# Stores of sums issued by ScalarE's queue instead of GpSimd's, in a two-block transformer kernel on one Trainium2 core

## The chip, the core and the metric

The kernel runs on one core of one Trainium2 chip. The core has five engines that run their own instruction streams and meet at semaphores: TensorE (PE: matmuls and transposes), VectorE (DVE), ScalarE (ACT), GpSimd (POOL) and SyncE (SP). SP, ACT and POOL can each issue DMA transfers, which then run beside the engines. The metric is the time of one execution on the device in microseconds (us), as the median of several runs; lower is better.

## What is computed

Two transformer blocks follow one another on one sequence of 256 tokens with 2048 features, in float32. The first has three mixers side by side (sparse, windowed and block attention), each with its own output matrix and gate, and an MLP; the second has two layers of two mixers each (differential and banded attention, then grouped and latent attention) with 256 more context tokens. What matters here is the shape of the large products:

```
h = rms_norm(x, norm_mix[layer])
... = jnp.split(h @ w_in[layer], SPLIT_POINTS, axis=-1)
y = jnp.einsum('bsmc,mcd->bsmd', branches, w_branch[layer])
x = x + jnp.sum(gate * y, axis=2) @ w_out[layer]
x = x + jnp.square(jax.nn.relu(h @ w_mlp_in[layer])) @ w_mlp_out[layer]
...
u = h @ e_w_in[i]          # second block, layer 0
u = h @ o_w_in[i]          # second block, layer 1
x = x + gate * (y @ w_o[l])
```

## The kernel before

**Steps and chunks.** All large products are `Step`s: 512 (or 472, 320) columns of a weight matrix, in chunks of two rows of 128 (`wcols`), against two or four tiles of 128 tokens. A step with two tiles uses two of the PSUM banks 0 to 3, one with four all of them. Float32 accuracy comes from three matmuls of split operands (lines 525, 529, 530): for each chunk SP loads `raw` (line 416, eight buffers), ScalarE copies it rounded to `w_hi` (`split_hi`, line 428, four buffers), VectorE subtracts to get `w_lo` (`split_lo`, line 434), and TensorE multiplies. ScalarE may write a `w_hi` buffer once TensorE has used the chunk four earlier, so both splitters can be up to three chunks ahead. A chunk is 12 matmuls with two tiles and 24 with four.

**Where the sums go.** Most projections (qkv, gates, in2, in3, and the small products QB and KVB) are steps of kind "store": ScalarE copies each tile's bank from PSUM to one of four buffers in SBUF (`act_evac`, line 577), and GpSimd stores the buffer to DRAM (`pool_store`, line 674), to U1, U2 or U3 (all read as U in the profile), GT, QB, KVB or MODP. Before the copy ScalarE waits for `acc_done` or `w_used` (TensorE has filled the bank) and for `stored` (the buffer's last store has landed); the copy's end raises `acc_free`, for which both GpSimd's store and TensorE's next use of the bank wait.

```
nc.scalar.activation(stage_bufs[bank][0:r, 0:s.width], acc[0:r, bank, 0:s.width],
                     e["func"], scale=e["scale"](tt) if callable(e["scale"]) else e["scale"])\
  .then_inc(acc_free[bank], 1)
```

**The order of the work.** Each engine's order is written out. `stream` (line 637) sets ScalarE's and VectorE's in a stage: the copies of the last step come behind the split of the third chunk of the next step in the stages named in `LATE`, and otherwise, and at each end of a stage, between the splits of the first and the second chunk of what follows. In the attention regions (`Region`, line 988) the products of a stage fill the gaps of small work units: TensorE makes scores, VectorE the maximum, ScalarE the exponential (`pb`, line 1242) and, two units later, a copy of the transposed result (`pt`, line 1251); `Region.act` puts the copies of a finished step ahead of a unit's exponential, and `Region.pool` GpSimd's stores at the same unit. The Silu of the later gates needs another table in ScalarE than the exponential, so there a table load stands on either side of the copies. Between in3 and what follows, the feed `p8q` (line 779, `a_hi`) comes right behind the copies. GpSimd has other work in the same queue: loads of gates and attention results for the next stage, reciprocal roots, and the saves of attention results.

Of the kernel before, what the change touches and what calls it, by code (L numbers as in the profile page):

```python
# [124 lines left out]
def two_blocks(nc, A, C, out):  # L125
    ctx = ExitStack()
    with ctx:
# [127 lines left out]
        stages = {}  # L255
# [9 lines left out]
        gates = [group(win, QKV1 + j * G, alternate(j == 0), x256, store(to(GT, j * G), ACT.Tanh, rms(2))) for j in range(12)]  # L265
# [299 lines left out]
        def act_evac(act, s):  # L565
            e = s.evac
            for bank, tt in s.tiles:
                if e["kind"] == "store":
                    wait_done(act, s, bank)
                    if s.put[bank]:  # L570
                        act.wait_ge(stored[bank], 16 * s.put[bank])
                    r = e["rows"]
                    if e.get("gates"):
                        c0 = e["gates"]
                        nc.scalar.activation(nsa_g[:, tt, :], acc[:, bank, c0:c0 + 24], ACT.Tanh, scale=rms(2)(tt))\
                          .then_inc(nsa_ready, 1)
# [3 lines that stand above are left out]
                elif e["kind"] == "relu2":  # L580
                    wait_done(act, s, bank)
                    if tt == 0:
                        act.wait_ge(ht_done, s.nth)
                    nc.scalar.activation(relu_t[:, tt, :], acc[:, bank, :], ACT.Relu, scale=rms(4)(tt))\  # L584
                      .then_inc(acc_free[bank], 1)

        def act_hidden(act, s):
            act.wait_ge(ht_done, s.nth + 1)
# [78 lines left out]
        def dve_stream(dve, st):  # L667
            stream(dve, st, split_lo, dve_evac, dve_hidden, "dve")

        def pool_store(pool, s):  # L670
            e = s.evac
            for bank, tt in s.tiles:
                pool.wait_ge(acc_free[bank], s.fill[bank] + 1)
                pool.dma_start(e["dst"](tt, s.width), stage_bufs[bank][0:e["rows"], 0:s.width])\  # L674
                    .then_inc(stored[bank], 16)
            if e.get("gates"):
                pool.wait_ge(nsa_ready, 2)
                pool.dma_start(AG.rearrange("(t p) n -> p t n", p=P), nsa_g[:, :, :]).then_inc(nsa_out, 16)

# [5 lines left out]
        def pool_stream(pool, st):  # L685
            if st.name == "branch":
                for s in st.steps:
                    q, n, m = s.nth, s.evac["n"], s.evac["m"]
                    if q >= 2:
                        pool.wait_ge(branch_tmp, 2 * (q - 1))  # L690
                    for tt in range(2):
                        pool.dma_start(gate_t[:, q % 2, tt, :], GT[tt * P:(tt + 1) * P, m * DM + n * G:m * DM + (n + 1) * G])\
                            .then_inc(gate_in[q % 2], 16)
                    if q == 3:
                        f2.turned(pool, f2.n - 1)
                        vec_bias(pool, 2)
                    vec_mods(pool, s)
                return
            for i, s in enumerate(st.steps):
                vec_mods(pool, s)  # L700
                if s.evac["kind"] == "relu2":
                    for bank, tt in s.tiles:
                        pool.wait_ge(acc_free[bank], s.fill[bank] + 1)
                        last = nc.gpsimd.tensor_tensor(relu_t[:, tt, :], relu_t[:, tt, :], relu_t[:, tt, :], ALU.mult)  # L704
                    last.then_inc(sq_done, 1)
                elif s.evac["kind"] == "store":
                    pool_store(pool, s)
                st.run_hooks("pool", i, 0, pool)

        def wait_stored(eng, upto):  # L710
# [277 lines left out]
        class Region:  # L988
# [100 lines left out]
            def pool(self, pool):  # L1089
                stored_here = []  # L1090
                for p in self.passes:
                    waiting = p.gate
                    for x in p.row_places + ["units"] + list(range(p.U + 3)):
                        for f in p.pool_parts.get(x, ()):
                            f(pool)
                        for s_ in self.finished(p, x):
                            pool_store(pool, s_)
                            stored_here.append(s_)
                        if waiting and (waiting[0] not in self.stage.steps or waiting[0] in stored_here):
                            for bank, _ in waiting[0].tiles:  # L1100
                                pool.wait_ge(stored[bank], 16 * (waiting[0].put[bank] + 1))
                            pool.dma_start(waiting[1], waiting[2]).then_inc(gate_there, 16)
                            waiting = None
# [1361 lines left out]
        def _(pool):  # L2465
# [28 lines left out]
            out2_roots(pool, 1, 0)  # L2494
            pool_stream(pool, stages["in3_low"])
            p8_pool(pool)
            pool_store(pool, stages["in3"].steps[0])
            p8_pool_norm(pool)
            for s_ in stages["in3"].steps[1:]:
                pool_store(pool, s_)  # L2500
            pool_stream(pool, stages["in3_g0"])
            C0.roots(pool)
            at3.pool(pool)
# [146 lines left out]
```

## Time and profile before

| | before |
|---|---|
| median of 3 runs | 3244.88 us (3236.37 to 3247.44) |
| the profiled execution | 3239.18 us, span 3237.4 us |
| granted clock of TensorE, mean | 0.984 |
| TensorE busy | 3137.8 us, 97% |
| VectorE busy | 1949.3 us, 60% |
| ScalarE busy | 1323.3 us, 41% |
| GpSimd busy | 234.1 us, 7% |
| stores issued on line 674, by destination | U 98, GT 24, KVB 16, QB 6, MODP 4: 148 |
| DMA moved | 620.53 MB, 192 GB/s in the mean |

The engines overlap, so the shares don't add up. A matmul's records overlap too, so that "97% busy" says that TensorE nearly always had a matmul under way and not that the array was at its peak. In the rows, L434 is line 434 of the kernel; `w_lo<-raw,w_hi` are the tensors written and read; ACTq and SPq are the queues in which these engines issue DMAs; "[0.26 <-DVE w_lo L434]" says that the engine was idle for 0.26 us before, until VectorE's line 434 released it. A granted clock of 1.00 is 2.4 GHz.

### The profile page before, as it was taken

What the parts mean: (1) busy time and instruction counts of PE and PEld (TensorE: products, weight loads), DVE (VectorE), ACT (ScalarE), POOL (GpSimd) and SP (SyncE); (2) the same over time, 40 slices, a digit from 0 to 9 for tenths busy, and PEclk for the clock granted to TensorE, in tenths of its full rate; (3) what the DMA queues carried; (4) which work ended last, traced back from release to release, by engine and by line L of the source; (5) the groups of instructions that cost most, each with busy time, mean ns of one, the idle gap of its engine ahead of it and who ended that gap; (6) DMA issues with size and microseconds to landing.
All of it is one profiled execution on the core that took longest, in us unless ns stands there. A gap on an engine that the chain in (4) does not pass through costs nothing.

```text
span 3237.4 us, 38936 instructions
## 1 busy us (share of the span) xinstructions
PE 3137.8 (97%) x14876; PEld 2553.0 (79%) x14876; DVE 1949.3 (60%) x2669; ACT 1323.3 (41%) x2084; POOL 234.1 (7%) x323
## 2 busy tenths in 40 slices
PE   8999999999999999999989999999999999999988
PEld 7887888888888888888878877777778878777666
DVE  5767555568769888887657433444445436355555
ACT  4443444443344343434543233333343324244553
POOL 1000000000001010100100000000001000020000
PEclk9999999999999999999999999999999999999999
DMA  8977855457768877897745522422435424464663
GB/s 243 346 255 258 269 177 168 143 181 270 258 206 271 270 254 261 267 257 254 235 145 176 163 80 94 142 65 101 129 103 198 133 83 134 162 215 128 211 231 133
DMA packets 319717, 620.53 MB, mean 192 GB/s; under 512 B 29515, under 2 KB 96456, under 8 KB 318636
## 3 DMA queue, kind: packets, MB, share of 16 engines
q1 hardware_dynamic: 296684, 544.74, 52.3%
q0 software_dynamic: 19600, 66.89, 6.0%
q10 hardware_dynamic: 3248, 6.42, 0.5%
q8 instruction: 119, 1.95, 0.3%
q14 instruction: 66, 0.54, 0.1%
HBM read 575.16 MB, written 49.08 MB: 193 GB/s over the span
## 4 chain that ended last, share of the span: by engine, by line
PE 87%; DVE 4%; DMA 4%; ACT 2%; issue 2%; POOL 1%; SPq 0%; ACTq 0%; POOLq 0%; DVEq 0%
PE acc L525 25%; PE acc L530 24%; PE acc L529 24%; PE acc L1180 4%; PE acc L1207 3%; PE acc L1195 2%; DVE w_lo L434 2%; DMA raw<-in_w_in 1%; PE acc L818 1%; PE acc L496 1%; PE acc L1184 1%; ACT w_hi L428 1%; PE acc L1164 1%; DMA QB<-stage 0%; PE acc L557 0%
## 5 line engine op out<-in xcount | busy, mean ns | idle before, releaser
L525 PE MATMUL acc<-w_hi,a_hi 128*128 128x512 f32 (+4 forms) x3800 | 1514.1, 398 | 22.8 <-DVE w_lo L434 13.7
L530 PE MATMUL acc<-w_hi,a_lo 128*128 128x512 f32 (+4 forms) x3800 | 1478.0, 389 | 0.0
L529 PE MATMUL acc<-w_lo,a_hi 128*128 128x512 f32 (+4 forms) x3800 | 1476.8, 389 | 0.0
L434 DVE TENSOR_TENSOR w_lo<-raw,w_hi 128x1024 fp32r<-128x1024 f32 (+3 forms) x826 | 984.5, 1208 | 439.2 <-ACT w_hi L428 427.5
L428 ACT ACTIVATE w_hi<-raw 128x1024 fp32r<-128x1024 f32 (+3 forms) x826 | 855.6, 1046 | 808.9 <-PE acc L530 757.4
L525 PEld LDWEIGHTS acc<-w_hi,a_hi 128*128 128x128 f32 x3800 | 723.7, 190 | 173.6 <-DVE w_lo L434 24.1
L530 PEld LDWEIGHTS acc<-w_hi,a_lo 128*128 128x128 f32 x3800 | 722.5, 190 | 146.2
L529 PEld LDWEIGHTS acc<-w_lo,a_hi 128*128 128x128 f32 x3800 | 723.9, 191 | 131.6 <-issue 1.0
L1321 DVE TENSOR_REDUCE at_st<-acc 128x1 f32<-128x256 f32 (+3 forms) x208 | 101.2, 487 | 423.0 <-PE acc L1180 282.2
L1242 ACT ACTIVATE pb<-acc,at_st 128x256 f32<-128x256 f32 (+3 forms) x208 | 108.3, 521 | 374.9 <-DVE at_st L1321 351.4
L469 DVE SCALAR_TENSOR_TENSOR lanes_b<-raw,ct,lanes_b 128x1024 f32<-128x1024 f32 x150 | 190.3, 1310 | 0.3 <-DMA raw<-in_w_mod 0.3
L469 DVE SCALAR_TENSOR_TENSOR lanes_c<-raw,ct,lanes_c 128x1024 f32<-128x1024 f32 x120 | 159.2, 1370 | 0.0
L674 POOL DMA_DIRECT2D U<-stage x98 | 53.3, 546 | 990.4 <-ACT stage L577 862.4
L1195 PEld LDWEIGHTS acc<-ident,pb 128*128 128x128 f32 (+1 forms) x528 | 63.4, 142 | 66.8 <-issue 58.9
L1251 ACT ACTIVATE pt<-acc 128x256 f32<-128x256 f32 (+3 forms) x208 | 89.5, 430 | 60.5 <-PE acc L1195 60.5
L1195 PE MATMUL acc<-ident,pb 128*128 128x128 f32 (+1 forms) x528 | 96.2, 281 | 10.7 <-ACT pt L1251 10.5
L577 ACT ACTIVATE stage<-acc 128x512 f32<-128x512 f32 (+2 forms) x100 | 55.1, 593 | 99.8 <-PE acc L530 86.4
L704 POOL TENSOR_TENSOR relu_t<-relu_t 128x512 f32<-128x512 f32 x32 | 56.4, 1772 | 495.5 <-ACT relu_t L584 495.5
L1298 DVE RECIPROCAL at_st<-at_st 128x1 f32<-128x1 f32 x208 | 33.9, 163 | 83.4 <-PE acc L1207 78.2
L859 DVE TENSOR_TENSOR a_lo<-acc,a_hi 128x512 fp32r<-128x512 f32 x76 | 51.9, 690 | 38.3 <-ACT a_hi L841 36.5
L1180 PE MATMUL acc<-kAT,qAT 64*128 64x512 f32 (+1 forms) x128 | 58.2, 534 | 0.0
L841 ACT ACTIVATE a_hi<-acc 128x512 fp32r<-128x512 f32 x44 | 25.6, 597 | 78.8 <-PE acc L818 78.8
(392 smaller groups left out, 1833.7 us busy)
## 6 DMA issues: line engine op xcount, KB each, us to landing
raw<-in_w_mod SPq DMA_DIRECT2D x192, 512.0 KB, 4.9
raw<-in_w_mlp_in SPq DMA_DIRECT2D x128, 512.0 KB, 4.1
raw<-in_w_mlp_out SPq DMA_DIRECT2D x128, 512.0 KB, 5.5
raw<-in_e_w_in SPq DMA_DIRECT2D x104, 512.0 KB, 5.1
raw<-in_w_in SPq DMA_DIRECT2D x96, 512.0 KB, 5.0
raw<-in_w_in SPq DMA_DIRECT2D x88, 472.0 KB, 5.7
raw<-in_w_o SPq DMA_DIRECT2D x64, 512.0 KB, 4.9
raw<-in_o_w_in SPq DMA_DIRECT2D x64, 512.0 KB, 4.3
```

The costliest lines, as they stand in the source:

```text
L428: nc.scalar.activation(w_hi[:, n % SPLITS, 0:size], raw[:, r % RAWS, 0:size], ACT.Copy)\
L434: nc.vector.tensor_tensor(w_lo[:, n % SPLITS, 0:size], raw[:, r % RAWS, 0:size], w_hi[:, n % SPLITS, 0:size].bitcast(F32), ALU.subtract)\
L469: nc.vector.scalar_tensor_tensor(out=t, in0=raw[:, vecs.raw[q] % RAWS, :], scalar=ct[:, k, v:v + 1], in1=bias_of(j)[:, :] if k == 0 else t ...
L525: nc.tensor.matmul(o, s.lhs(0, kt, tt), wh, start=kt == 0, stop=False)
L529: nc.tensor.matmul(o, s.lhs(0, kt, tt), wl, start=False, stop=False)
L530: last = nc.tensor.matmul(o, s.lhs(1, kt, tt), wh, start=False, stop=end)
L1180: last = nc.tensor.matmul(acc[:, bank, 0:w.keys], w.q[x], w.k[x], start=x == 0, stop=x == n - 1 and w.bias is None)
L1195: last = nc.tensor.transpose(acc[0:kk, bank, x * P:(x + 1) * P], self.pb[:, v % self.npb, x * P:x * P + kk], ident[:, :])
L1207: last = nc.tensor.matmul(acc[:, self.obanks[v % len(self.obanks)], 0:P], self.pt[0:kk, v % 2, x, :], vt, start=x == 0, stop=x == len(w.v) ...
L1242: nc.scalar.activation(self.pb[:, v % self.npb, 0:w.keys], acc[:, 4 + v % 2, 0:w.keys], ACT.Exp, bias=st[:, 0:1], accum_out=st[:, 1:2]).th ...
L1251: nc.scalar.activation(self.pt[0:kk, v % 2, 0:n, :], acc[0:kk, self.tbanks[v % len(self.tbanks)], 0:n * P].rearrange("p (n t) -> p n t", n ...
L1321: ins = nc.vector.tensor_reduce(m, acc[:, 4 + v % 2, 0:w.keys], AX.X, ALU.max, negate=True)
```

## The change

The stores of a step are issued by ScalarE, behind all the copies of that step, and no longer by GpSimd. The waits, the transfers and the buffers are the same. GpSimd keeps the one extra store of a step with `gates`. The new function stands ahead of the lines of before, so that line n of `Region` and of all below is n + 4 afterwards; the new store is line 593.

```diff
                     nc.scalar.activation(relu_t[:, tt, :], acc[:, bank, :], ACT.Relu, scale=rms(4)(tt))\
                       .then_inc(acc_free[bank], 1)
+            if e["kind"] == "store":
+                act_store(act, s)
+
+        def act_store(act, s):
+            e = s.evac
+            for bank, tt in s.tiles:
+                act.wait_ge(acc_free[bank], s.fill[bank] + 1)
+                act.dma_start(e["dst"](tt, s.width), stage_bufs[bank][0:e["rows"], 0:s.width])\
+                    .then_inc(stored[bank], 16)
...
-        def pool_store(pool, s):
-            e = s.evac
-            for bank, tt in s.tiles:
-                pool.wait_ge(acc_free[bank], s.fill[bank] + 1)
-                pool.dma_start(e["dst"](tt, s.width), stage_bufs[bank][0:e["rows"], 0:s.width])\
-                    .then_inc(stored[bank], 16)
-            if e.get("gates"):
+        def pool_gates(pool, s):
+            if s.evac.get("gates"):
                 pool.wait_ge(nsa_ready, 2)
                 pool.dma_start(AG.rearrange("(t p) n -> p t n", p=P), nsa_g[:, :, :]).then_inc(nsa_out, 16)
...
-                    pool_store(pool, s)
+                    pool_gates(pool, s)
...
-                            pool_store(pool, s_)
+                            pool_gates(pool, s_)
```

The two direct calls behind stage in3 on GpSimd are renamed in the same way.

ScalarE where stage qkv ends and qkv_end begins, before. `w_hi` of 128x928 belongs to qkv_end, whose first chunk is split ahead of the copies; in brackets are the semaphores that the row waits for.

```order
L428 ACTIVATE w_hi<-raw 128x928 [waits w_used,landed0]
L577 ACTIVATE stage<-acc,small 128x472 [waits stored2,acc_done2]
L577 ACTIVATE stage<-acc,small 128x472 [waits stored3,w_used]
L428 ACTIVATE w_hi<-raw 128x928 [waits w_used,landed2]
L428 ACTIVATE w_hi<-raw 128x928 [waits w_used,landed3]
```

The same place afterwards:

```order
L428 ACTIVATE w_hi<-raw 128x928 [waits w_used,landed0]
L577 ACTIVATE stage<-acc,small 128x472 [waits stored2,acc_done2]
L577 ACTIVATE stage<-acc,small 128x472 [waits stored3,w_used]
L593 DMA U<-stage 128x472 [waits acc_free2]
L593 DMA U<-stage 128x472 [waits acc_free3]
L428 ACTIVATE w_hi<-raw 128x928 [waits w_used,landed2]
L428 ACTIVATE w_hi<-raw 128x928 [waits w_used,landed3]
```

Two issues, each with a wait for ScalarE's own copy, now stand ahead of the split of the second chunk.

ScalarE in the second attention region, at a gate step with four tiles and Silu, before:

```order
L577 ACT_TABLE_LOAD [waits stored2]
L577 ACTIVATE stage<-acc 128x512 [waits acc_done2]
L577 ACTIVATE stage<-acc 128x512 [waits stored3,acc_done3]
L577 ACTIVATE stage<-acc 128x512 [waits stored0,acc_done0]
L577 ACTIVATE stage<-acc 128x512 [waits stored1,w_used]
L1241 ACT_TABLE_LOAD [waits at_t_done]
L1241 ACTIVATE at_st<-sinkB,at_st 128x1 [waits at_m_done]
```

And afterwards:

```order
L577 ACTIVATE stage<-acc 128x512 [waits stored1,w_used]
L593 DMA U<-stage 128x512 [waits acc_free2]
L593 DMA U<-stage 128x512 [waits acc_free3]
L593 DMA U<-stage 128x512 [waits acc_free0]
L593 DMA U<-stage 128x512 [waits acc_free1]
L1245 ACT_TABLE_LOAD [waits at_t_done]
L1245 ACTIVATE at_st<-sinkB,at_st 128x1 [waits at_m_done]
```

Four issues stand between the last copy and the table load for the exponential (line 1241 before, 1245 now).

ScalarE where the products QB end and KVB begin, before:

```order
L577 ACTIVATE stage<-acc 128x512 [waits stored0,acc_done0]
L577 ACTIVATE stage<-acc 128x512 [waits stored1,w_used]
L577 ACTIVATE stage<-acc 128x512 [waits stored2,acc_done2]
L577 ACTIVATE stage<-acc 128x512 [waits stored3,acc_done3]
L577 ACTIVATE stage<-acc 128x512 [waits stored0,acc_done0]
L577 ACTIVATE stage<-acc 128x512 [waits stored1,w_used]
L1242 ACT_TABLE_LOAD [waits at_t_done]
```

And afterwards:

```order
L593 DMA QB<-stage 128x512 [waits acc_free0]
L593 DMA QB<-stage 128x512 [waits acc_free1]
L577 ACTIVATE stage<-acc 128x512 [waits stored2,acc_done2]
L577 ACTIVATE stage<-acc 128x512 [waits stored3,acc_done3]
L577 ACTIVATE stage<-acc 128x512 [waits stored0,acc_done0]
L577 ACTIVATE stage<-acc 128x512 [waits stored1,w_used]
L593 DMA KVB<-stage 128x512 [waits acc_free2]
L593 DMA KVB<-stage 128x512 [waits acc_free3]
L593 DMA KVB<-stage 128x512 [waits acc_free0]
L593 DMA KVB<-stage 128x512 [waits acc_free1]
L1246 ACT_TABLE_LOAD [waits at_t_done]
```

The store of bank 2 now follows the copy of bank 1, which itself waits until the store of QB from bank 1 has landed.

## Rows read from the trace of the kernel before

**Rows 1.** The page, part 1: busy time and its share of the span.
```profile
PE 3137.8 (97%) x14876; PEld 2553.0 (79%) x14876; DVE 1949.3 (60%) x2669; ACT 1323.3 (41%) x2084; POOL 234.1 (7%) x323
```

**Rows 2.** Waits of TensorE: line, releaser, us in total, times, longest.
```profile
PE acc L525 <- DVE w_lo L434: 13.7, 18, 2.4
...
PE acc L525 <- ACT stage L577: 8.4, 8, 2.7
```

**Rows 3.** Line 674: duration min/median/max; its waiters; then DMA issues, KB, us to landing.
```profile
L674 POOL DMA_DIRECT2D U<-stage x98: 539/540/642, 40.3 to 3042.4; - x98
...
  ACT stage L577: 12.4, 7
...
out<-XR SPq DMA_DIRECT2D x4, 512.0 KB, 3.9
...
QB<-stage POOLq DMA_DIRECT2D x6, 256.0 KB, 6.2
```

**Rows 4.** Issues on the queues of ScalarE and SP; timeline of ScalarE, 79 to 82.
```profile
L1352 ACTq DMA_DIRECT2D onehot_t<-const_onehot x1: 467/467/467, 1.2 to 1.2; - x1
...
L1116 SPq DMA_DIRECT2D kA<-U x4: 501/1045/1685, 1835.3 to 2086.2; - x4
...
79.38 1.00 ACT L428 ACTIVATE w_hi<-raw 128x944 fp32r<-128x944 f32 x1 [1.58 <-PE acc L530]
79.40 0.86 ACTq L1444 DMA_DIRECT2D BROW<-BREV  x1
81.95 0.99 ACT L428 ACTIVATE w_hi<-raw 128x944 fp32r<-128x944 f32 x1 [1.58 <-PE acc L530]
```

**Rows 5.** Timelines around 264, then TensorE at 43 and 2861.
```profile
263.10 0.65 ACT L577 ACTIVATE stage<-acc,small 128x472 f32<-128x472 f32 x1 [0.63 <-PE acc L530]
263.66 3.57 ACT L428 ACTIVATE w_hi<-raw 128x928 fp32r<-128x928 f32 x4
...
264.05 0.54 POOL L674 DMA_DIRECT2D U<-stage  x1 [0.75 <-ACT stage L577]
...
265.84 0.48 PE L525 MATMUL acc<-w_hi,a_hi 128*128 128x464 f32 x1 [0.26 <-DVE w_lo L434]
...
43.35 0.48 PE L525 MATMUL acc<-w_hi,a_hi 128*128 128x472 f32 x1 [0.40 <-DVE w_lo L434]
...
2861.03 0.50 PE L525 MATMUL acc<-w_hi,a_hi 128*128 128x512 f32 x1 [0.18 <-DVE w_lo L434]
```

**Rows 6.** Timelines of ScalarE and TensorE, 2347 to 2353, a step with Silu.
```profile
2347.28 2.07 ACT L577 ACTIVATE stage<-acc 128x512 f32<-128x512 f32 x4
2349.37 1.28 ACT L1241 ACT_TABLE_LOAD   x1
...
2352.98 0.63 PE L1195 MATMUL acc<-ident,pb 128*128 128x128 f32 x4 [2.21 <-ACT pt L1251]
```

**Rows 7.** Timelines of ScalarE and TensorE, 2830 to 2833.
```profile
2830.40 1.08 ACT L779 ACTIVATE a_hi<-acc 128x512 fp32r<-128x512 f32 x2
...
2832.57 0.63 PE L770 MATMUL acc<-ident,lr 128*128 128x128 f32 x4 [2.01 <-DVE a_lo L787]
```

**Rows 8.** Timelines where QB and KVB are made, ScalarE, then TensorE.
```profile
2885.53 0.60 ACT L577 ACTIVATE stage<-acc 128x512 f32<-128x512 f32 x1 [0.82 <-PE acc L530]
...
2892.88 1.28 ACT L1242 ACT_TABLE_LOAD   x1
...
2872.89 0.47 PE L525 MATMUL acc<-w_hi,a_hi 128*128 128x512 f32 x1 [1.34 <-ACT stage L577]
...
2898.55 0.47 PE L525 MATMUL acc<-w_hi,a_hi 128*128 128x512 f32 x1 [0.44 <-ACT stage L577]
```

**Rows 9.** Stretches of 10 us (PEclk is the granted clock); TensorE at 2953.
```profile
2350.00:2360.00 10.00, 7.79 (x45) 6.19 (x44) 4.01 (x11) 5.23 (x14) 0.33 (x1) 1.00 0.22 80
...
2950.00:2960.00 10.00, 7.24 (x24) 5.43 (x25) 1.44 (x3) 5.21 (x7) 1.07 (x2) 0.83 0.96 301
...
2953.42 0.75 PE L525 MATMUL acc<-w_hi,a_hi 128*128 128x512 f32 x1 [2.69 <-ACT stage L577]
```

More of the change, by code:

```diff
@@ L2496, in _ @@
             p8_pool(pool)
-            pool_store(pool, stages["in3"].steps[0])
+            pool_gates(pool, stages["in3"].steps[0])
             p8_pool_norm(pool)
             for s_ in stages["in3"].steps[1:]:
-                pool_store(pool, s_)
+                pool_gates(pool, s_)
             pool_stream(pool, stages["in3_g0"])
```

## The prediction

> **What bounds the kernel now.** I read the page first. TensorE is busy for 3137.8 us, 97% of the span [rows 1], so only 100 us of it are idle, and anything that makes or ends waits moves the time only where TensorE itself then waits longer or shorter. The list of waits by engine comes next: TensorE's largest is for the low half of a weight chunk, w_lo, which VectorE makes behind ScalarE's w_hi (13.7 us in 18 waits), and it waits 8.4 us in 8 cases for a copy of sums out of PSUM [rows 2]. So ScalarE matters where its lead over TensorE is used up. The view of the line that issues the stores shows what moves: 98 stores to U2 and its like, and 50 more of the same line to other tensors, 148 in all, each 0.54 us of GpSimd; only 12.4 us of ScalarE's copies waited for a store to land [rows 3]. Last I read the timelines of ScalarE, VectorE and TensorE around the copies.
>
> **What is removed.** 148 issues of 0.54 us are 80 us of GpSimd [rows 3]. GpSimd ends nothing on TensorE's path in those stretches, it sat idle before the stores. Worth 0. Its remaining work (loads, roots) no longer queues behind stores; I count nothing for it, and the last part below says where it could show.
>
> **What is added, per step.** ScalarE now issues a step's stores behind all its copies of the step. The only price of an issue on ScalarE's queue is that of small loads: 0.467 us [rows 4]. The bounds: 0 from below, since the large issue at 79.40 ran beside the w_hi at 79.38, and the next w_hi at 81.95 still waited for TensorE [rows 4]; 1.045 us from above, the median of a 512 KB issue on SP that comes right behind another one [rows 4]. I take 0.47: same queue, though fewer rows. The issue also waits for the copy's own end: GpSimd's issue at 264.05 began 0.30 us after the copy of 263.10 + 0.65 ended [rows 5]. In a step with two tiles the first issue runs beside the second copy, and the second one costs 0.30 + 0.47 from the end of that copy. Since the next split began 0.09 us before the end, ScalarE is late by **0.86 us**. In a step with four tiles the issues start with the last copy (about 2348.77, which ends at 2349.35) and take 4 x 0.47 = 1.88, until 2350.65; the table load that stood at 2349.37 [rows 6] comes **1.3 us** later.
>
> **Where ScalarE's lead covers it.** In the long streams of weights ScalarE is a chunk ahead by four buffers: it idles 1.58 us before each w_hi, waiting for TensorE [rows 4]. A delay of 0.86 or 1.3 us once in 8 chunks is swallowed. This covers most of the steps, those of qkv, the gates of the first attention and the three of in2 among them.
>
> **Where it does not.** (a) Where one stage follows another, the copies stand ahead of the split of the second chunk, and that chunk is needed one chunk (12 matmuls, 2.6 us) after the last tile is done. At 263.66 ScalarE begins the split right behind the copy, and at 265.84 TensorE has waited 0.26 for w_lo [rows 5]: no lead is left. I count six such places with two tiles, the first at 43.35 and the last at 2861.03 [rows 5], with 266, 287, 2707 and 2766 between (waits of VectorE's w_lo or of work behind it). 6 x 0.86 = **5.2 us**.
> (b) Steps with four tiles and no lead: the two last gate steps but one with Silu, where the exponential waits for the table and TensorE at 2352.98 has waited 2.21 us for pt [rows 6] (the next such step, 69 us on, is alike); the switch to in3 at 2742; and the a_hi at 2830.40, which starts as the last copy ends and for which TensorE waits 2.01 us [rows 7]. 4 x 1.3 = **5.2 us**.
> (c) The steps that make QB and KVB, where a step has one or two chunks. One two-tile step puts 0.9 us ahead of a w_hi that VectorE's rotations of q wait for. The step whose first copy is at 2885.53 and behind whose last the table load stands, at 2892.88 [rows 8], issues its four stores there: 1.3. Its first bank, copied at 2885.53, is now stored behind the last, 6 to 7 us later than before, and the copies of the next steps wait for such landings; I add 1.8 for that. **4.0 us** (0.9 to 9).
> (d) TensorE's clock. The gap of 2.21 us before 2352.98 left the granted clock at 1.00 (2.4 GHz), while the stretch with the gap of 2.69 us at 2953.42 has 0.83 over 10 us, that is 1.2 GHz in part of it, and costs 0.17 x 10 = 1.7 us [rows 6, 9]. With 1.3 us more, the gap at 2353 would be 3.5 us and its twin much the same, longer than the one that had the drop. 2 x 1.7 = **3.4 us** (0 to 3 more drops, 0 to 8.5).
>
> **What may come back.** A store on the hardware queue may land sooner. QB's stores on GpSimd's queue took 6.2 us in the median, while a store of twice the size on SP's, at the quiet end of the program, took 3.9 [rows 3]. TensorE waited 1.34 and 0.44 us behind copies that such landings held up, at 2872.89 and 2898.55 [rows 8]. I take these 1.8 us, say **-2 us**; the ends are 0 (the difference is traffic, not the queue) and -8.4, all of TensorE's waits for copies [rows 2].
> The Trainium skill (DMA: Bandwidth & Descriptors, Latency and other measured facts) gives a first byte at 0.6 us for such queues and 1 us for GpSimd's; by that estimate each landing comes only 0.4 us sooner and the term would be about -1. The same page (Issuing engines are not separate DMA queues) says that the choice of the engine saves only sequencer time at the issue; by that the term would be 0. No row here has the same store on both queues.
>
> **The sum.** 5.2 + 5.2 + 4.0 + 3.4 - 2 = +15.8 us. The profiled execution took 3239.2 us, so it would be 3255.0; the median of the three runs lies 5.7 above it, at 3244.9, so I forecast **3260.7 us**, +0.5%.
>
> **Rivals.** *The issue is hidden (not slower).* The sequencer of ScalarE runs ahead of its datapath, as at 79.40 [rows 4]; if the stores cost ScalarE only the 0.30 us of waiting for its own copy, the two-tile steps cost 6 x 0.2, the four-tile ones about 0, (c) 1, no clock is lost, and -2 comes back: 3245. It decides where the issue plus the wait stays under 0.3 us. For it: that row. Against it: the store must wait for the copy to end, which the issue at 79.40 did not have to do, so nothing runs beside it.
> *The landing is what counts (faster).* If stores land in 3.9 us instead of 6.2, ScalarE's 12.4 us of waits [rows 3] go almost whole, with the chains of loads behind them. Even with all 8.4 us of rows 2 gained and the issue hidden, this gives 3236 to 3238. Against it: TensorE shares only 1.8 us of those waits [rows 8].
> *The queue is clogged (much slower).* Four issues of 256 KB in a row meet SP's loads, and each takes about 1.05 us as the kA row of SP does [rows 4]. Then a four-tile step costs 1.3 + 4 x 0.58 = 3.6 us and a two-tile one 0.86 + 0.58 = 1.4: 6 x 1.4 + 4 x 3.6 + 8 for (c) + 5 clock drops of 1.7 - 2 = +37: 3282.
>
> **How the numbers follow.** A measurement of this kernel can tell about 0.3%, 9.7 us, from no change. The forecast with its bounds (+8 to +26) has 0.58, the hidden issue (-3 to +8) 0.25, the clogged queue 0.09, the faster landing 0.08. The part of the forecast under +9.7 us (0.04) goes to no change. That gives 0.08 faster, 0.29 same, 0.63 slower. The range is 3243 to 3277: it leaves out the faster case and the clogged one, and the outer parts of the others.
>
> **What would show each step.** Right: ScalarE's queue with 148 issues of 0.4 to 0.6 us; at the place of 263.66 the split some 0.9 us behind its copy's end and TensorE's wait for w_lo at 1.1; the table load of 2349.37 1.3 us behind the last copy and the wait for pt at 2352.98 at 3.5, with a granted clock under 1.00 in the stretch; the wait of a_lo at 2832.57 at 3.3. TensorE's total of waits for w_lo rises from 13.7 to about 19. Wrong: issues that begin before the copy ends, or gaps before these rows as they were; then (a) and (b) fall. If the waits for QB and KVB shrink from 12.4 us to under 6 the landing term was too small. If GpSimd's load of the last gates, which was queued behind stores, lands earlier and TensorE's small waits near 2500 go, that is a gain that I count at nothing.

## The result, and the profile after

The changed kernel takes **3263.78 us**, the median of 5 runs (3261.04 to 3265.73), against 3243.06 us for the kernel before (median of 5, 3236.37 to 3247.44). The ratio is 1.0065, 95% interval 1.005 to 1.0079: some 21 us slower. I had forecast 3260.7, in a range of 3243 to 3277. The size came out; much of the way there did not, as the trace shows. The profiled execution took 3261.04 us (span 3259.2), 21.9 more than the one before.

The page after, by engine. TensorE's work is the same to 0.5 us against [rows 1], and GpSimd is down to 175 instructions, as 148 issues have left it:

```profile
PE 3137.3 (96%) x14876; PEld 2553.4 (78%) x14876; DVE 1948.5 (60%) x2669; ACT 1327.2 (41%) x2084; POOL 155.3 (5%) x175
```

TensorE's waits by what ended them (in all, times, longest), the lines that answer to [rows 2]:

```profile
PE acc L525 <- DVE w_lo L434: 31.2, 19, 15.1
PE acc L1199 <- ACT pt L1255: 11.8, 11, 3.0
PE acc L525 <- ACT stage L577: 8.4, 7, 2.7
...
PE acc L774 <- DVE a_lo L791: 4.1, 2, 3.3
```

The wait for w_lo has grown from 13.7 to 31.2 us, and 15.1 of that is one wait. I had expected 19 in all. The new line of the stores, now on ScalarE's queue (min/median/max ns), with the time to landing of all 148:

```profile
L593 ACTq DMA_DIRECT2D U<-stage x98: 326/329/16247, 41.4 to 3064.8; - x98
L593 ACTq DMA_DIRECT2D GT<-stage x24: 326/327/400, 320.4 to 705.1; - x24
L593 ACTq DMA_DIRECT2D KVB<-stage x16: 326/412/1203, 2912.9 to 2939.3; - x16
...
DMA to landing us min/median/max: 1.9/4.4/20.4
```

An issue costs 0.33 us (0.41 in the median to KVB), not the 0.467 that I took from a small load [rows 4]. But the longest took 16.25 us. Here is ScalarE around it:

```profile
79.43 0.86 ACTq L1448 DMA_DIRECT2D BROW<-BREV  x1
...
84.55 1.00 ACT L428 ACTIVATE w_hi<-raw 128x944 fp32r<-128x944 f32 x1 [1.58 <-PE acc L530]
85.78 0.66 ACT L577 ACTIVATE stage<-acc,small 128x472 f32<-128x472 f32 x1 [0.23 <-PE acc L530]
87.07 0.66 ACT L577 ACTIVATE stage<-acc,small 128x472 f32<-128x472 f32 x1 [0.63 <-PE acc L530]
87.07 20.46 ACTq L593 DMA_DIRECT2D U<-stage  x2
107.63 3.63 ACT L428 ACTIVATE w_hi<-raw 128x944 fp32r<-128x944 f32 x4 [19.91 <-issue]
```

Two issues stand in front of the next w_hi for 20.46 us, the first for 16.25 and the second for 4.17 ("issue" as the releaser says that ScalarE waited for nothing that the profile shows; its own two issues fill that time). TensorE works on to 94.75 on what is split, stops for 15.10 us, and comes back at 1.2 GHz in part: the granted clock was 0.50 and 0.81 in the two stretches from 100 to 120 us, where it was 1.00 before (the last three rows: stretch, TensorE's busy time, granted clock, DMA share, GB/s):

```profile
109.85 0.76 PE L525 MATMUL acc<-w_hi,a_hi 128*128 128x472 f32 x1 [15.10 <-DVE w_lo L434]
...
90.00:100.00 10.00, 4.75 (x23) 0.84 0.82 302
100.00:110.00 10.00, 0.15 (x1) 0.50 0.81 237
110.00:120.00 10.00, 10.00 (x39) 0.81 1.00 305
```

This store stands right behind the load BROW<-BREV (6144 KB, issued at 79.43 on the same queue), of which the prediction used the row [rows 4] and drew no consequence. The places that it did name are all there, smaller:

```profile
277.33 0.48 PE L525 MATMUL acc<-w_hi,a_hi 128*128 128x464 f32 x1 [0.83 <-DVE w_lo L434]
...
2367.60 0.66 PE L1199 MATMUL acc<-ident,pb 128*128 128x128 f32 x2 [2.98 <-ACT pt L1255]
...
2440.18 0.63 PE L1199 MATMUL acc<-ident,pb 128*128 128x128 f32 x4 [2.44 <-ACT pt L1255]
...
2852.34 0.87 PE L774 MATMUL acc<-ident,lr 128*128 128x128 f32 x3 [3.35 <-DVE a_lo L791]
...
2881.92 0.50 PE L525 MATMUL acc<-w_hi,a_hi 128*128 128x512 f32 x1 [0.75 <-DVE w_lo L434]
```

They stood at 0.26 [rows 5], 2.21 [rows 6], 1.98 (its twin at 2422), 2.01 [rows 7] and 0.18 [rows 5]: +0.57, +0.77, +0.46, +1.34 and +0.57.

### The profile page after: what moved, and what is told of

The parts are those of the page before. It is cut to its first block, busy times and chain, and to the rows that moved or that the text cites. A ratio compares the mean times of both kernels' runs of the same rounds, so it can differ in the third digit from the quotient of the medians.

```text
span 3259.2 us, 38933 instructions
## 1 busy us (share of the span) xinstructions
PE 3137.3 (96%) x14876; PEld 2553.4 (78%) x14876; DVE 1948.5 (60%) x2669; ACT 1327.2 (41%) x2084; POOL 155.3 (5%) x175
## 3 DMA queue, kind: packets, MB, share of 16 engines
q1 hardware_dynamic: 296684, 544.74, 51.9%
## 4 chain that ended last, share of the span: by engine, by line
PE 86%; issue 5%; DVE 4%; ACT 2%; DMA 2%; ACTq 1%; POOL 0%; SPq 0%; POOLq 0%; DVEq 0%
PE acc L525 25%; PE acc L530 24%; PE acc L529 24%; PE acc L1184 4%; PE acc L1211 3%; PE acc L1199 2%; DVE w_lo L434 2%; PE acc L496 1%; PE acc L822 1%; ACTq L593 1%; PE acc L1188 1%; ACT w_hi L428 1%; PE acc L1168 1%; DMA raw<-in_w_in 1%; PE acc L557 0%
## 5 line engine op out<-in xcount | busy, mean ns | idle before, releaser
L863 DVE TENSOR_TENSOR a_lo<-acc,a_hi 128x512 fp32r<-128x512 f32 x76 | 51.9, 690 | 41.9 <-ACT a_hi L845 40.3
L1211 PE MATMUL acc<-vA,pt 128*128 128x128 f32 x384 | 53.3, 275 | 0.0
```

Of the source, the lines that this page charges most:

```text
L1211: last = nc.tensor.matmul(acc[:, self.obanks[v % len(self.obanks)], 0:P], self.pt[0:kk, v % 2, x, :], vt, start=x == 0, stop=x == len(w.v) ...
```

## The experiments

Each ratio is against the kernel before on the same chip; in us it is the ratio's excess times that kernel's median (3243.1 for the change; 3240.9, 3241.1 and 3242.2 for the others). The intervals reach 0.001 to 0.0018 to either side, 3 to 6 us, and a difference of two rows is less certain than either.

| run | ratio to before | interval | in us |
|---|---|---|---|
| the change | 1.0065 | 1.005 to 1.0079 | +21.1 |
| e1, big load on GpSimd | 1.0037 | 1.0024 to 1.005 | +12.0 |
| c1, before with the same | 1.0026 | 1.0016 to 1.0036 | +8.4 |
| e2, one step's stores back | 1.0026 | 1.0014 to 1.0037 | +8.4 |
| e3, that step alone moved | 1.0046 | 1.0033 to 1.0059 | +14.9 |
| e4, e2 with stores behind the split | 1.002 | 1.001 to 1.0031 | +6.5 |
| e5, first projection and gates only | 1.0013 | 1.0004 to 1.0023 | +4.2 |
| e6, in2 only | 1.0007 | 0.9996 to 1.0018 | +2.3 |
| e7, in3 and behind only | 1.0006 | 0.9995 to 1.0017 | +1.9 |
| e8, big load in eight pieces | 1.007 | 1.0056 to 1.0084 | +22.7 |
| e9, before with the same | 1.004 | 1.0025 to 1.0055 | +13.0 |
| e10, pieces, stores behind the split | 1.0064 | 1.0049 to 1.0079 | +20.8 |
| e11, e8 with each store in halves | 1.029 | 1.0272 to 1.0307 | +94.0 |

### One step put back, and that step alone

In e2 the two stores of step 1 of the first projection, those of the 20.46 us, go back to GpSimd, with a semaphore of their own; in e3 they alone are moved. Waits on `stored` then count both semaphores. The same code makes both (in e3 soft(s) is `s is not ...`):

```
+        def soft(s):
+            return s is stages["qkv"].steps[1]
...
-            if e["kind"] == "store":
+            if e["kind"] == "store" and not soft(s):
                 act_store(act, s)
...
-                    .then_inc(stored[bank], 16)
+                    .then_inc((soft_stored if soft(s) else stored)[bank], 16)
...
         def pool_gates(pool, s):
+            if soft(s):
+                act_store(pool, s)
```

> The changed kernel, with the stores of a single step (two stores of 236 KB, step 1 of the first projection, those that took 20.46 us to issue) back on GpSimd, with a semaphore of their own; the other 146 stay on ScalarE, and so does the 6144 KB load. Theory (same queue): ScalarE has nothing to issue while its queue is full, the next step's stores come 22 us later, when it has drained: 3253 to 3255 us, with GpSimd's two issues at 0.54 us each. If the queue is full for longer, the step after it pays instead, 1 to 10 us. Rival (traffic): GpSimd's two issues take as long as ScalarE's did, but nothing waits behind them; also 3253 to 3255. Rival (sum of many small costs, and the stall of 15 us only swallowed a lead that is regained later): 3260 to 3264 us.

> The kernel before, with only that one step's two stores moved to ScalarE, behind the 6144 KB load on the same queue; 146 stores stay on GpSimd. Theory (same queue): the whole unforeseen part comes back from these two instructions: two issues of 16 and 4 us, a wait of TensorE of about 15 us less the 3 us that it waits there now, a clock drop of 20 us in part, and in all 9 to 11 us above the kernel before: 3252 to 3254 us. Rival (many small costs): 3242 to 3245 us.

Measured: +8.4 us for e2, so two of the 148 stores make 12.7 of the 21.1 (by the intervals of the two rows, give or take some 6); and +14.9 (10.7 to 19.1) for e3, where 9 to 11 were expected. Issues of e2's stores on both queues, then ScalarE's queue in e3 and TensorE behind it:

```profile
L611 POOL DMA_DIRECT2D U<-stage x2: 543/555/567, 88.4 to 89.5; - x2
L611 ACTq DMA_DIRECT2D U<-stage x96: 322/337/7608, 41.3 to 3056.8; - x96
```

```profile
86.62 21.50 ACTq L611 DMA_DIRECT2D U<-stage  x2
...
110.44 0.76 PE L543 MATMUL acc<-w_hi,a_hi 128*128 128x472 f32 x1 [16.14 <-DVE w_lo L452]
```

In e2 GpSimd issued these stores in 0.54 to 0.57 us at 88 us, in the stretch in which ScalarE's queue took 16.25 in the change: the traffic on the DMA engines does not block every issue. That it is the queue, and not ScalarE, the next section shows. And e2 still has an issue of 7.61 us: the second one of the next step, at 109.8, 29 us behind the load, right behind one of 0.32 us (TensorE waits 2.93 for w_lo there). I read this as a queue with no room left, which empties only as the load moves; how much it holds was not measured. The DMA view of before, in the windows 84 to 88, 124 to 128 and 132 to 136 us (packets, MB, share of the engines), shows ScalarE's queue, q10, and SP's weights, q1, at about half each soon after the load's issue at 79.40 and still side by side 40 us on; at 132 q10 is gone:

```profile
q10 hardware_dynamic: 359, 0.74, 51.9%
q1 hardware_dynamic: 299, 0.54, 43.4%
...
q1 hardware_dynamic: 365, 0.84, 67.0%
q10 hardware_dynamic: 204, 0.41, 28.9%
...
q1 hardware_dynamic: 655, 1.39, 96.5%
```

So a store on this queue was held until some 28 us (the change, e3) to 37 us (e2) after the load's issue. The Trainium skill (DMA: Bandwidth & Descriptors, Issuing engines are not separate DMA queues) says that initiating DMAs on several engines "will only save the time on the sequencer it takes to initiate the DMA". By that the move would cost ScalarE no more than 148 times an issue of 0.33 us; the runs show that the time to initiate can be 16.2 us, by what stands unmoved in the same engine's queue.

### The big load on another queue

e1 is the change, c1 the kernel before, each with this load on GpSimd:

```
             pool.wait_ge(brev_out, 16)
+            src = BREV[0]
+            pool.dma_start(BROW[:, :, :], bass.AP(src.tensor, 0, [[G, 24], [0, P], [1, G]])).then_inc(bt_out, 16)
...
-            act.wait_ge(brev_out, 16)
-            src = BREV[0]
-            act.dma_start(BROW[:, :, :], bass.AP(src.tensor, 0, [[G, 24], [0, P], [1, G]])).then_inc(bt_out, 16)
```

> The changed kernel, with the one issue of the 6144 KB load BROW<-BREV moved from ScalarE's queue to GpSimd's, right behind the store of BREV it reads; all 148 stores of sums stay on ScalarE. Theory (same queue): the two store issues behind 87.07 took 16.25 and about 4.2 us because the big load had filled ScalarE's own queue. Then here every store issue takes 0.3 to 0.4 us, TensorE's wait of 15.1 us for w_lo near 109.85 is gone with its clock drop, and the time is 9 to 11 us under the changed kernel: 3253 to 3255 us, still 10 above the kernel before. Rival (traffic): the 16 DMA engines are full of that load whoever issues it, and any store issue blocks in that stretch. Then ScalarE's issue there still takes over 10 us and the time stays at 3262 to 3266 us.

> The kernel before, with the same move of the 6144 KB load to GpSimd's queue; its stores are on GpSimd too. A control: if the theory of the same queue holds, GpSimd's next store issues near 87 us, which stand behind it, may take long, but no weight split is queued behind them there, so TensorE loses at most a wait for a free copy buffer: 3240 to 3247 us, no difference from the kernel before that can be told. If moving the load is worth something in itself (other than through the stores), this shows it, and the run before is to be read against this one. Rival (traffic): the same 3240 to 3247 us.

The edit moves the load in time too: GpSimd issues it as soon as its source is there, at 53.6 us in e1 and 54.2 in c1, where ScalarE issued it at 79.4. So the stores to look at in e1 are those of step 0, 14 us behind the load. GpSimd's issue of the load, its queue (q0) from 66 to 70 us, and ScalarE's two stores there:

```profile
53.61 1.67 POOL L1438 DMA_DIRECT2D BROW<-BREV  x1 [1.61 <-DMA BREV<-brev_t]
...
q0 software_dynamic: 179, 0.70, 48.4%
...
67.11 1.18 ACTq L593 DMA_DIRECT2D U<-stage  x2
```

The load has 48.4% of the engines, about as much as in before from 84 to 88 us, and ScalarE issues the two stores in 0.33 and 0.50 us. With the load in another queue neither its traffic nor ScalarE's own issuing blocks. None of the 148 issues took over 2.21 us, and the wait of 15 us is gone. (The next step's stores, two in 0.87 us at 102.44, prove less: from 98 to 102 us q0 has 1.1% of the engines, so the load had moved.)

But e1 gained less than expected, and c1 lost 8.4 us, which neither theory had. On GpSimd's queue the load, issued 25 us earlier, had 37 to 53% of the engines in every window of 4 us from 62 to 94 us in e1 and c1, the weights came late, and TensorE waited with the stores on either engine. First c1, then e1:

```profile
89.99 0.76 PE L525 MATMUL acc<-w_hi,a_hi 128*128 128x472 f32 x1 [5.88 <-DVE w_lo L434]
```

```profile
88.74 0.48 PE L525 MATMUL acc<-w_hi,a_hi 128*128 128x472 f32 x1 [3.65 <-DVE w_lo L434]
```

Whether the other queue or the earlier start costs these 8.4 us is not told apart. Against its own control e1 is 3.6 us slower, which the intervals don't part from zero.

### The rest, in three parts

e5, e6 and e7 move the stores of one region each (soft(s) is true for all others, and for the blocked step).

> Only the stores of the first projection and the gates (without the one step behind the 6144 KB load) are issued by ScalarE, right behind the copies as in the change; those of in2, in3 and what comes after stay on GpSimd. Theory (price at each stage switch): four places, 0.6 each at about 43, 266 and 287 us and 0.9 near 324: 2 to 4 us over the kernel before, ratio 1.0006 to 1.0012. Rival (it is spread evenly, some traffic effect): its share of the +8.4 by number of stores, 42 of 146: about 2.4 us, so this run separates little by itself, but the next two do.

> Only the stores of in2 and its rest (52 stores in four-tile steps) are issued by ScalarE. Theory: only the two gate steps with the table load lose (+0.77 and +0.46 in TensorE's waits for pt), with one clock drop of 1.7 us in one of the two, and 0.3 near 2500: +2 to +4 us, ratio 1.0006 to 1.0012. By my prediction's own terms it would be 2 x 1.3 + 3.4 = 6.0. Rival (even share): 52 of 146 of 8.4, 3.0 us.

> Only the stores of in3 and what stands beside the third attention (QB, KVB, the last gates, MODP; 52 stores) are issued by ScalarE. Theory: the switches into and out of in3 (about 0.5, 0.7, 0.6 and 0.6), a_lo +1.3, the wait for QB's q (+0.6) and the one near 3070 (+1.4), against 0.4 + 0.9 + 0.8 gained in waits behind copies: +3 to +5 us, ratio 1.0009 to 1.0016, and the three parts add up to 7 to 12. Rival (QB and KVB gain from earlier landing): under +1.

They came to +4.2, +2.3 and +1.9, in all 8.4, the same as e2; the sum is certain to some 6 us only. Singly e6 and e7 can't be told from no change; their traces can, since each named wait grows in the run that moves its region, and stays in the others:

| TensorE's wait (us) | before | e5 | e6 | e7 |
|---|---|---|---|---|
| w_lo, stage switch at 266 | 0.26 | **0.83** | 0.26 | 0.26 |
| w_lo, stage switch at 287 | 0.22 | **0.79** | 0.22 | 0.22 |
| pt, at 2353 | 2.21 | 2.21 | **2.98** | 2.21 |
| pt, at 2422 | 1.98 | 1.98 | **2.42** | 1.98 |
| a_lo, at 2833 | 2.01 | 2.01 | 2.01 | **3.35** |
| w_lo, at 2861 | 0.18 | 0.18 | 0.18 | **0.75** |

e5 also holds a blocked issue of 7.98 us in the step after the big load's, for which TensorE waits 3.30 us (the load's own waits there, 0.77 and 1.82 us in before, are 2.59).

### The issue behind the work that TensorE wants

e4 is e2 with each step's stores put off: in the streams behind the next split, in the attention regions behind a place's own exponential, split and copy of pt.

```
-                act_store(act, s)
+                late.append(s)
...
+        def flush(act):
+            while late:
+                act_store(act, late.pop(0))
...
         def split_hi(act, s, c):
+            split_one(act, s, c)
+            flush(act)
```

> All stores of sums on ScalarE but those of the one step behind the 6144 KB load, which stay on GpSimd as in the run with that step back. The other 146 issues are put off: in the streams of weights behind the next w_hi split, in the attention regions behind the place's own work (its exponential, its split and its copy of pt). Theory (the issues cost only where TensorE's next chunk or pt stands behind them): the waits for w_lo at the stage switches go back to 0.2 to 0.4 us, the waits for pt to 2.2 and 2.0, the one for a_lo to 2.0; what is left is landing later than now: 0 to 3 us over the kernel before, against +8.4 (ratio 1.0026) with the issues in front. Rival (landing): stores that start later hold the copies of the next steps and the loads that read the sums; the waits behind copies (8.4 us) and for q, k and v grow, and +5 to +10 stays. Rival (contention or background): +8 stays with no wait at the places named.

+6.5 us, which its interval does not part from e2's 8.4. The waits that the prediction had named went back, all but one (a_lo: the stores of that step are still issued ahead of p8's work). But one that was 0.75 before became 5.26:

```profile
263.03 0.48 PE L547 MATMUL acc<-w_hi,a_hi 128*128 128x464 f32 x1 [0.26 <-DVE w_lo L456]
...
2363.36 0.95 PE L1230 MATMUL acc<-ident,pb 128*128 128x128 f32 x4 [2.21 <-ACT pt L1288]
...
2847.72 0.52 PE L805 MATMUL acc<-ident,lr 128*128 128x128 f32 x3 [3.36 <-DVE a_lo L822]
...
2032.76 0.66 PE L1230 MATMUL acc<-ident,pb 128*128 128x128 f32 x2 [5.26 <-ACT pt L1288]
```

There the stores themselves are waited for. SP loads q and k from what they write, ahead of its raw weights; w_hi waits 7.88 us for such a weight, and pt stands behind w_hi. SP's row, and ScalarE's:

```profile
2021.47 0.37 SPq L1151 DMA_DIRECT2D qA<-U  x1
...
2023.13 10.65 SPq L434 DMA_DIRECT2D raw<-in_e_w_in  x9
```

```profile
2016.57 0.81 ACTq L622 DMA_DIRECT2D U<-stage  x2
...
2031.07 1.06 ACT L450 ACTIVATE w_hi<-raw 128x1024 fp32r<-128x1024 f32 x1 [7.88 <-DMA raw<-in_e_w_in]
2032.03 0.58 ACT L1288 ACTIVATE pt<-acc 128x512 f32<-128x512 f32 x1
```

From the step's first copy to SP's load of qA it takes 5.8 us before (2008.84 to 2014.64), 5.9 in the changed kernel, and 8.4 here (2013.05 to 2021.47): the delay of the issues, handed on. My rival for this run, landing, was half right: one place, 4.5 us. With that place left alone e4 would come to some +2, an estimate (6.5 less 4.5, which takes the wait of the profiled execution, 3254.95 us, to be there in the median of 3246.87 too); that was not tried.

### The load in pieces

e8 (the change), e9 (before) and e10 (the change with stores behind the split) issue the big load as eight of 768 KB, one a step (behind the third split of a step; in e10 behind the fifth):

```
-        stages["qkv"].hook("act", 2, 0, lambda act: setup_bias_tiles(act))
+        for k in range(8):
+            stages["qkv"].hook("act", 2 + k, 2, lambda act, k=k: setup_bias_tiles(act, k))
...
-            act.dma_start(BROW[:, :, :], bass.AP(src.tensor, 0, [[G, 24], [0, P], [1, G]])).then_inc(bt_out, 16)
+            act.dma_start(BROW[3 * k:3 * k + 3, :, :], bass.AP(src.tensor, 3 * k * G, [[G, 3], [0, P], [1, G]]))\
+                .then_inc(bt_out, 16)
```

> The changed kernel (all 148 stores on ScalarE, right behind their copies), with the 6144 KB load in eight pieces of 768 KB, still on ScalarE's queue: one behind the stores of each step from the third to the tenth of the first projection, some 19 us apart. Theory (a store's issue waits when too much stands unmoved in ScalarE's own queue): the load of 6144 KB took from 84 to about 130 us at its share; a piece takes about 6 us and is gone before the next stores. No store issue over 1.5 us in that region, no wait of 15 us. Then the change costs what its other steps cost: +8.4 us (ratio 1.0026) less the 7.6 us issue that was still there in that run (worth about 1.5 us to TensorE) and less the waits of 2.6 us and the clock drop that the big load caused before: +3 to +6 us over the kernel before, ratio 1.001 to 1.002. Rival (any store behind any load in that queue waits until that load has been issued into the engines in full): eight issues of 2 to 5 us, and +8 or more.

> The kernel before (stores on GpSimd) with the same eight pieces on ScalarE's queue: the control for the run above. TensorE's waits of 0.77 and 1.82 us at 128.9 and 133.6 go, and the clock of 0.83 beside them (1.7 us): 3 to 4 us under the kernel before, ratio 0.9987 to 0.9991. If the pieces collide with the weights as the whole did, no difference. The two runs of this pair give the price of the stores' move without the queue: 6 to 8 us.

> All 148 stores on ScalarE, each put off behind the next split or the place's own work as in the run with the stores behind the split, and the load in eight pieces behind the fifth split of a step. It takes away both costs that the study has found. Theory: no long issue, the waits for w_lo, pt and a_lo as in the kernel before: -3 to +1 us against the kernel before, ratio 0.999 to 1.0003, and 4 to 7 us under the run with the pieces alone. Rival (landing or traffic of the hardware queue): +3 to +6 stays.

All three missed, by 16 to 20 us from the nearer end of the theory. The queue behaved as the theory said: in e8 no store's issue took over 1.49 us. But the pieces cost 13 us in themselves, also with the stores on GpSimd: between 140 and 200 us a weight's load landed in 15.6 us in the median where it took 5.0 before, and TensorE waited 1.6 us again and again. DMA issues of weights in that stretch (KB, median us to landing), before and in e9, then the share of ScalarE's queue in e9 and one of TensorE's waits:

```profile
raw<-in_w_in SPq DMA_DIRECT2D x24, 472.0 KB, 5.0
```

```profile
raw<-in_w_in SPq DMA_DIRECT2D x20, 472.0 KB, 15.6
...
q10 hardware_dynamic: 983, 2.00, 8.6%
...
183.03 0.48 PE L525 MATMUL acc<-w_hi,a_hi 128*128 128x472 f32 x1 [1.64 <-DVE w_lo L434]
```

It isn't the sum of the traffic: the engines moved less in that stretch (264 GB/s against 298). The trace shows what the pieces did. The theory gave a piece 6 us; in e9 each takes 20 to 22 us from its first packet to its last, so that from 90 to 276 us one is nearly always under way, while the whole load was through in 47.5 us (83.3 to 130.7 in before). By the packet records ScalarE's queue hardly ever has more than three packets in flight in e9, and mostly four to eight with the whole load. The edit cut more than the size: a piece is 3 blocks of 128 rows where the whole was 24. It looks as if a piece ran on three of the 16 engines, at its share of them, and the weights waited for these three; but the trace does not name the engine of a packet, and pieces of another shape, which would test it, were not run. So e8 to e10 are no test of a small load as such. Read against its control, e8 gives the price of the stores without the blocked queue: 22.7 - 13.0 = 9.7 us, give or take some 6. e10 is 1.9 us under e8, not told apart; it too has the pt wait near 2036 us, 4.82 us.

### The price doubled

e11 is e8 with each store issued as two halves by rows, 296 issues:

```
+                h = e["rows"] // 2
+                for r in (0, h):
+                    act.dma_start(e["dst"](tt, s.width)[r:r + h, :], stage_bufs[bank][r:r + h, 0:s.width])\
+                        .then_inc(stored[bank], 16)
```

> As the run with the load in eight pieces, but each store is issued as two halves by rows (296 issues instead of 148, the same bytes): the suspected cost doubled. Theory (price of the issue at places without lead): a two-tile step pays one more issue after its last copy (0.33 us), a four-tile step up to four more (1.3 us): 6 x 0.33 + 4 x 1.3 + 1 to 2 for QB and KVB = 8 to 9 us over the run with the pieces alone, if the table loads and pt stand behind them all; TensorE's waits at 2353 and 2422 go from about 3.0 and 2.5 to about 4.3 and 3.8. Rival (what counts is the wait for the copy's end, not the issue): 0 to 2 us over it. Rival (landing): shorter transfers land sooner, under it.

It is 71 us over e8, not 8. The first reason is in the row of the issues: a half costs 0.615 us, almost twice what a whole store does, so a tile takes 1.23 us of the queue and not 0.33. TensorE's waits grew with it, for w_lo from 27.9 us in e8 to 44.6 and for pt from 11.6 to 28.6 in all; and TensorE was busy for 26 us more (3142.2 to 3168.6), at a mean granted clock of 0.974 against 0.983, so the longer waits came with a lower clock:

```profile
L595 ACTq DMA_DIRECT2D U<-stage x196: 452/615/3037, 41.5 to 3140.2; - x196
...
46.28 0.64 PE L525 MATMUL acc<-w_hi,a_hi 128*128 128x472 f32 x1 [2.24 <-DVE w_lo L434]
...
2409.79 0.45 PE L1201 MATMUL acc<-ident,pb 128*128 128x128 f32 x1 [5.84 <-ACT pt L1257]
...
2913.39 0.87 PE L776 MATMUL acc<-ident,lr 128*128 128x128 f32 x3 [6.54 <-DVE a_lo L793]
```

At the first place the last issue ends 1.02 us after the last copy's start in e8 and 2.28 us after it in e11; TensorE's wait there goes from 0.99 to 2.24. So 1.26 us more of the queue is 1.25 us more of waiting: at these places the issue's time reaches TensorE one for one. At the four-tile places it is 0.90 x 4 = 3.6 us of queue for 2.8 (pt, 3.03 to 5.84) and 3.2 us (a_lo, 3.34 to 6.54). That the wait for the copy's end is what counts, a rival, falls with this. The Trainium skill (DMA: Bandwidth & Descriptors, Rules for kernel authors) advises one 128-partition transfer over two of disjoint halves, since both use the same engines. The run agrees with the advice and adds a reason, the dearer issue; which engines the halves used it does not show.

## Why the prediction was right, and where it was not

**Right in sign and in what carries the places.** The places of (a), (b) and (d) were read from the timelines, and each named wait grew. The reading that TensorE's lead is nil at stage switches and behind the Silu steps holds in e5, e6, e7 and e11.

**(a) 5.2 us forecast, 3.4 measured** in the growth of TensorE's waits: 0.59 (at 43), 0.57, 0.55, 0.51, 0.57, 0.57. The size of the issue was off, 0.33 for 0.47: the row of a small load was the wrong one to take it from.

**(b) 5.2 forecast, 4.2 measured:** 0.77, 0.46, 1.58 at the switch to in3 and 1.34 at a_lo (0.86 of it came back at 2760 and 0.21 behind a_lo). With an issue of 0.33 four of them are 1.3 us, less what stands beside the last copy.

**(c) 4.0 forecast, 0.7 measured** from 2861 to 2953 as the shift between the traces, 20.89 to 21.57. TensorE's waits behind the copies went from 1.34 to 0.96 and from 0.44 to 1.08, and for q's rotation from 2.04 to 2.66. Banks stored late were given 1.8 us; TensorE's two waits for copies rose from 1.78 to 2.04 together.

**(d) 3.4 forecast, 3.4 in the profile, by luck.** The prediction had one drop of 1.7 us at each of two places. One place, behind a gap of 2.98 us, had two stretches of 10 us at 0.83, which is 0.17 x 20 = 3.4 us; the other, with a gap of 2.44, kept 1.00 (stretch, TensorE's busy time, granted clock, DMA share, GB/s):

```profile
2360.00:2370.00 10.00, 6.84 (x35) 0.83 0.46 157
2370.00:2380.00 10.00, 10.00 (x43) 0.83 0.01 2
```

In e2 and in e6 the first place kept 1.00 behind gaps of 2.96 and 2.98 us, and the second lost 1.7 us behind 2.46 and 2.42. So this term comes and goes from execution to execution, and the length of the gap did not decide it.

**The landing term, -2 forecast, is nil.** Stores took 4.4 us to land in the median against 4.0, and ScalarE's copies waited 10.4 us for them against 12.4: ScalarE's issue hardly brought them in sooner, if at all.

**What was missing** is the largest piece: 12.7 us by the medians (21.1 less 8.4), or by rows 15.1 of waiting and 0.19 x 10 of clock, less the 2.6 us of waits and 1.7 of clock that the load cost before in the same stretch. The step of the prediction that failed is the sentence that qkv's steps are covered by a lead of four buffers. That lead was worth 7.7 us here (TensorE worked on from 87.07 to 94.75), enough for 0.86, and it was applied to all steps without asking what else stood in the queue to which they were moved. The row of the 6144 KB load was even quoted, as proof that an issue runs beside ScalarE's work. The rival of a clogged queue put the clog in SP's loads and in every step, 1.05 us each; it was ScalarE's own queue, one step, and 20 us.

So the sum of the named terms was 15.8 and came to 8.4 (e2, and e5 to e7 together; 9.7 by e8 less e9, 3.6 by e1 less c1), with intervals that reach from nothing to 16; the rows above give 3.4 + 4.2 + 0.7 + 3.4 = 11.7, less the 1.1 that came back in (b). The forecast was within 3.1 us of the time because two errors offset, which is luck: named terms too large, by 4 to 12 us in these figures, and one large term not seen. TensorE's waits for w_lo, of which I expected 19 us in all, are 17.6 in e2.

**The two traces.** From 53 to 277 us the trace of the change falls behind by 9.9 us only, where the stretch of the load makes 12.7. The difference is the clock elsewhere in that span: before had 0.83 from 50 to 60 us and 0.66 from 200 to 210, where the change had 1.00 and, from 210 to 220, 0.83. That is 3.4 us that before lost more; 12.7 - 3.4 + 0.57 (the longer wait at 277) = 9.9.

**Left open:** how much ScalarE's queue holds before an issue waits; what of c1's 8.4 us is the earlier start; and whether pieces of another shape would slow the weights.

## What to carry to other kernels

Before a DMA is moved to another engine's queue, list what that queue already holds near each of its places, by bytes: a large load behind which small stores are issued can make the engine wait for much of the time in which the load drains (20 of some 50 us here), and all its compute with it. Then price the issue only where the engine's lead is used up; there it reaches the bound engine nearly one for one, and moving the issue behind the wanted work takes that wait away (e4), but can make a new one where somebody waits for what is stored. And a lead of n buffers covers a delay up to its own length, so ask for the longest delay, not the usual one.

## What the hardware showed that I had not expected

- A store of 236 KB on ScalarE's queue was issued in 0.33 us, or in 16.25 us with a 6144 KB load 8 us ahead of it in the same queue, while GpSimd's issue in the same stretch took 0.54 to 0.57 us. The last store to be held up was taken 28 us behind the load's issue in the change and 37 us in e2, with the load's data still moving (in the kernel before q10 has 28.9% of the engines at 124 to 128 us, 45 us behind the issue). With the load on GpSimd's queue, at 48.4% of the engines, ScalarE issued two stores in 0.33 and 0.50 us.
- The same store as two of 64 rows costs 0.615 us for each issue instead of 0.326 for one of 128 rows.
- A 6144 KB load beside SP's weights had 37 to 53% of the engines from 62 to 94 us on GpSimd's queue (e1, c1), and 28.7 to 51.9% from 84 to 128 us on ScalarE's (before). In c1, with GpSimd's stores, TensorE waited for 8.6 us in three waits.
- Eight loads of 768 KB (3 x 128 rows) in place of one of 6144 KB (24 x 128 rows) took 20 to 22 us each, with hardly ever more than three packets in flight, where the whole took 47.5 us; the landing of SP's weights rose from 5.0 to 15.6 us, at a lower total rate.
